# Scaling and biasing the attention scores on TensorE, and spreading the chunk inversion over four quadrants

## The reference

```
# RWKV-7, per head and direction, step by step
sa = S a_t
S  = S * w_t + sa b_t^T + v_t k_t^T
y_t = S r_t

# attention of one head, latent queries; context queries have keys of context only and no bias
s_loc = q k_r^T * scale + bias          # 64-wide rows, a mask of -1e9 outside a window
s_ctx = q k_ctx^T * scale
p = softmax([s_loc, s_ctx]);  o = p [v_r; v_ctx]
```

## Time and profile before

| | |
|---|---|
| Median of three runs | 2026.12 us (2019.57 to 2027.88) |
| The profiled execution's own time | 2030.75 us |
| Its span in the trace | 2028.6 us |
| TensorE busy | 1905.9 us, 94% |
| VectorE, ScalarE, GpSimd busy | 1001.8, 939.8 and 944.0 us (49%, 46%, 47%) |
| Mean granted TensorE clock | 0.982 of full speed |
| The chain that ended last | TensorE 79%, VectorE 9%, ScalarE 4% |

### The profile page before, as it was taken

How to read it: one execution, slowest core, us unless ns; L and a number is a source line. 1 busy time by engine, 2 the same in 40 slices (tenths; PEclk the granted TensorE clock), 3 DMA queues, 4 the chain that set the end, 5 groups by cost and what they waited for, 6 DMA issues and landing times.

```text
span 2028.6 us, 41739 instructions
## 1 busy us (share of the span) xinstructions
PE 1905.9 (94%) x17940; PEld 1718.9 (85%) x17940; DVE 1001.8 (49%) x1516; ACT 939.8 (46%) x1766; POOL 944.0 (47%) x767
## 2 busy tenths in 40 slices
PE   6899999999999989999988999999999998999997
PEld 2887878797899879999947878787879997899996
DVE  2574747475611255552057657475745133555502
ACT  4554645454533454443345555364554334544432
POOL 1434426170666626666416153342516664466663
PEclk9999999999999989999989999999999999999998
DMA  7314232232443314434453141413224432244442
GB/s 291 101 50 143 64 117 94 89 115 86 135 124 122 120 63 124 124 122 127 123 204 124 50 140 55 136 65 125 87 88 156 125 125 83 94 125 125 125 125 73
DMA packets 65414, 231.52 MB, mean 114 GB/s; under 512 B 7376, under 2 KB 11856, under 8 KB 64592
## 3 DMA queue, kind: packets, MB, share of 16 engines
q1 hardware_dynamic: 59040, 215.21, 33.3%
q10 hardware_dynamic: 6192, 13.66, 1.9%
HBM read 223.58 MB, written 5.26 MB: 113 GB/s over the span
## 4 chain that ended last, share of the span: by engine, by line
PE 79%; DVE 9%; ACT 4%; issue 3%; POOL 2%; DMA 2%; ACTq 1%; SPq 0%; DVEq 0%; POOLq 0%
PE psz L471 57%; PE psw L471 20%; DVE work L1360 3%; ACT work L954 3%; DMA ring<-in_w 2%; POOL ringlo L1735 1%; DVE work L1369 1%; PE psz L479 1%; PE psw L479 1%; ACT whi L954 1%; DVE rstd L1369 1%; DVE part L1360 1%; DVE work L1363 1%; POOL work L1771 1%; DVE work L1366 0%
## 5 line engine op out<-in xcount | busy, mean ns | idle before, releaser
L1735 POOL TENSOR_TENSOR ringlo<-ring,whi 128x512 fp32r<-128x512 f32 x608 | 811.1, 1357 | 756.7 <-ACT whi L954 756.7
L471 PE MATMUL psz<-hhi,whi 128*128 128x386 f32 x1696 | 587.1, 346 | 23.2 <-POOL ringlo L1735 14.5
L471 PE MATMUL psz<-hlo,whi 128*128 128x386 f32 x1696 | 577.6, 341 | 0.0
L471 PE MATMUL psz<-hhi,ringlo 128*128 128x386 f32 x1696 | 576.4, 340 | 0.0
L954 ACT ACTIVATE whi<-ring 128x1024 fp32r<-128x1024 f32 x304 | 320.2, 1053 | 133.4 <-PE psz L471 125.1
L471 PE MATMUL psw<-work 64*64 64x64 f32 (+4 forms) x9024 | 348.8, 232 | 17.6 <-issue 9.1
L471 PEld LDWEIGHTS psw<-work 64*64 64x64 f32 (+2 forms) x9024 | 294.5, 137 | 73.1 <-issue 55.6
L471 PEld LDWEIGHTS psz<-hhi,whi 128*128 128x128 f32 x1696 | 321.0, 189 | 36.1 <-issue 18.9
L471 PE MATMUL psz<-part,whi 128*128 128x386 f32 x1344 | 346.6, 339 | 3.2 <-DVE work L1360 1.5
L471 PEld LDWEIGHTS psz<-hlo,whi 128*128 128x128 f32 x1696 | 322.9, 190 | 2.1
L471 PEld LDWEIGHTS psz<-hhi,ringlo 128*128 128x128 f32 x1696 | 321.0, 189 | 0.0
(11 more groups left out here) (107 smaller groups left out, 1725.2 us busy)
## 6 DMA issues: line engine op xcount, KB each, us to landing
ring<-in_w SPq DMA_DIRECT2D x400, 512.0 KB, 3.5
pk<-in_pk ACTq DMA_DIRECT2D x8, 832.0 KB, 4.4
const<-in_const SPq DMA_DIRECT2D x1, 1795.0 KB, 10.0
work<-in_x SPq DMA_DIRECT2D x1, 1544.0 KB, 6.8
work<-in_x ACTq DMA_DIRECT2D x1, 1544.0 KB, 6.5
out_x<-work ACTq DMA_DIRECT2D x1, 1544.0 KB, 5.5
work<-out_x ACTq DMA_DIRECT2D x1, 1544.0 KB, 9.8
out_x<-work SPq DMA_DIRECT2D x4, 386.0 KB, 2.3
```

The source lines that it names most:

```text
L471: ins = nc.tensor.matmul(out, a, b, start=start, stop=stop, skip_group_check=True)
L1735: L.do(G.tensor_tensor(out, a, b, op), S[sig] if sig else None)
```

## The change

Two changes are made together.

**Attention.** The bias is added by a product of the identity with the bias, accumulated on the scores in PSUM, so that the scores need not be copied to SBUF: VectorE takes the negated maximum of bank 4 in one operation and ScalarE takes the exponential from bank 4. Bank 4 is free for the next job's scores only then (`p_ready` in the place of `s_ready`). The rows are no longer scaled: ScalarE multiplies the identity by the inverse row sums (`rdiag`, one buffer of 128x128, signal `ridiag_ready`), and TensorE turns the exponentials by a product with that matrix.

**Inversion.** Head 1's matrices in `tvv`, `g0` and `art` lie in swapped halves, so that the four products of an `x` (two heads, two chunks) take four different quadrants, and the loops over `x` and `hb` change places. The product waits for both heads at once. Step 3 of level 5 has a diagonal form in both heads. The transpose of a level is in three pieces: 128x384 for head 0 and two of 64x384 across the halves for head 1 (`across`); before level 1, `across` is added behind the transpose. The `art` copies on ScalarE are three in the place of one. `values(1)` and `powers(3)` on ScalarE change places.

```diff
                             else:
-                                pe.wait_ge(*at_of("s_ready", p, j - 1))
+                                pe.wait_ge(*at_of("p_ready", p, j - 1))
...
-                                mm(w(4, P, 256), q, nk[rows(hb), LAT:TP], sig="sc_done")
+                                mm(w(4, P, 256), q, nk[rows(hb), LAT:TP], True, False)
+                                if j == 1:
+                                    pe.wait_ge(*at_of("bias_ready", p, 0))
+                                a = PK["bias"] + 384 * hb + (P if kind == 1 else 0)
+                                mm(w(4, P, 256), ident, pk[:, a:a + 256], False, True, "sc_done")
...
-                            pe.wait_ge(*at_of("pn_ready", p, j))
+                            pe.wait_ge(*at_of("ridiag_ready", p, j))
...
-                                tr(w(5, i * P, P), scores[j % 2][:, i * P:(i + 1) * P], "pt_done" if i == n - 1 else None)
+                                mm(w(5, i * P, P), scores[j % 2][:, i * P:(i + 1) * P], rdiag,
+                                   sig="pt_done" if i == n - 1 else None)
...
-                            for hb in range(2):
-                                pe.wait_ge(*at_of("x_ready", p, 0 if lv == 1 else 2 * (lv - 2) + hb + 1))
-                                for x in range(6):
+                            pe.wait_ge(*at_of("x_ready", p, 0 if lv == 1 else 2 * (lv - 2) + 2))
+                            for x in range(6):
+                                for hb in range(2):
                                     for c in range(2):
-                                        mm(psw[hc(c), g_bank(lv, hb), CH * x:CH * x + CH], au[hc(c), hb, x, 0, 0:CH],
+                                        mm(psw[hc(c ^ hb), g_bank(lv, hb), CH * x:CH * x + CH], au[hc(c), hb, x, 0, 0:CH],
...
+                                        e = c ^ hb
+                                        o_ = psw[hc(e if lv == LEVELS - 1 else c), x_bank(lv, hb), CH * x:CH * x + CH]
+                                        mm(o_, a_[hc(e), hb, x, :], b_[hc(e), hb, x, :],
+                                           sig="xt_done" if (x, c) == (5, 1) else None)
...
-                            if i < 6:
-                                act.wait_ge(*at_of("sc_done", p, i))
-                                run(scores[i % 2][:, 0:P], w(4, 0, P), sig="sctx_ready")
+                            if 1 <= i <= 6:
+                                j = i - 1
+                                act.wait_ge(*at_of("ri_ready", p, j))
+                                run(rdiag, ident, ACT.Copy, "ridiag_ready", scale=ri[:, j % 2:j % 2 + 1])
...
-                        powers(3)
                         values(1)
+                        powers(3)
...
+                    def across():
+
+                        for c in range(2):
+                            flip(tvv[hc(1 - c), 1:2], xv[hc(c), 1:2], "tv_ready" if c else None)
...
-                                ts(s_[:, 0:n], s_[:, 0:n], ri[:, j % 2:j % 2 + 1], sig="pn_ready")
...
-                                flip(tvv, xv, "tv_ready")
+                                flip(tvv[:, 0:1], xv[:, 0:1])
+                                across()
```

More of the change, by code:

```diff
@@ L258, in trunk @@
         st = wk(3 * 256).rearrange("p (n s d v) -> p n s d v", n=3, s=2, d=2)
-        fin = wk(2 * 64).rearrange("p (d v) -> p d v", d=2)
+        rdiag = wk(P)
         lwal, lgl = wk(TP), wk(TP)
@@ L767, in _ @@
                                     ada_steps(2)
[L768 to L773, removed]
+                            pe.wait_ge(*at_of("gl_ready", p, lv - 1))
+                            pe.wait_ge(*at_of("tv_ready", p, lv - 1))
+                            a_, b_ = (gg, tvv) if lv == LEVELS - 1 else (tvv, gg)
+                            for x in range(6):
+                                for hb in range(2):
                                     for c in range(2):
[L775 to L776 removed]
+                                        e = c ^ hb
+                                        o_ = psw[hc(e if lv == LEVELS - 1 else c), x_bank(lv, hb), CH * x:CH * x + CH]
+                                        mm(o_, a_[hc(e), hb, x, :], b_[hc(e), hb, x, :],
+                                           sig="xt_done" if (x, c) == (5, 1) else None)
                             if lv <= 4:
@@ L784, in _ @@
                         freed(zb + 14)
-                        for hb in range(2):
-                            pe.wait_ge(*at_of("tv_ready", p, 4 + hb))
-                            for x in range(6):
+                        pe.wait_ge(*at_of("tv_ready", p, 6))
+                        for x in range(6):
+                            for hb in range(2):
                                 for c in range(2):
[L789 to L792, removed]
+                                    mm(psw[hc(c), hb, CH * x:CH * x + CH], tvv[hc(c ^ hb), hb, x, :],
+                                       art[hc(c ^ hb), x // 3, x % 3, rows(hb)], sig="wm_done" if (x, c) == (5, 1) else None)
+                        for x in range(6):
+                            for hb in range(2):
                                 for c in range(2):
-                                    mm(psw[hc(c), 2 + hb, CH * x:CH * x + CH], tvv[hc(c), hb, x, :],
-                                       g0[hc(c), hb, x, :], sig="u_done" if (x, c) == (5, 1) else None)
+                                    mm(psw[hc(c), 2 + hb, CH * x:CH * x + CH], tvv[hc(c ^ hb), hb, x, :],
+                                       g0[hc(c ^ hb), hb, x, :], sig="u_done" if (x, c) == (5, 1) else None)
                         retain(2)
@@ L1119, in powers @@
                                 act.wait_ge(*at_of("mx_ready", p, i))
-                                s_ = scores[i % 2][:, 0:384 if JOBS[i][1] else P]
-                                run(s_, s_, ACT.Exp, "p_ready", bias=mx[:, i % 2:i % 2 + 1], accum_out=rs[:, i % 2:i % 2 + 1])
+                                n = 384 if JOBS[i][1] else P
+                                run(scores[i % 2][:, 0:n], w(4, 0, n), ACT.Exp, "p_ready", bias=mx[:, i % 2:i % 2 + 1], accum_out=rs[:, i % 2:i % 2 + 1])
                         def retain(i):
@@ L1207, in _ @@
                                     seen(zi)
-                                    run(art[:, d], z(zi, 384).rearrange("p (t c) -> p t c", t=3), free=zi)
+                                    a = z(zi, 384).rearrange("p (t c) -> p t c", t=3)
+                                    run(art[:, d, :, rows(0)], a[:, :, rows(0)])
+                                    run(art[hc(0), d, :, rows(1)], a[hc(1), :, rows(1)])
+                                    run(art[hc(1), d, :, rows(1)], a[hc(0), :, rows(1)], free=zi)
                             elif lv in (2, 3):
@@ L1372, in pred, with flip @@
                         L.do(V.copy_predicated(out, mask, data), S[sig] if sig else None)
-                    def flip(out, a, sig):
-                        L.do(V.transpose(out.rearrange("p h x c -> p (h x c)"), a.rearrange("p h x c -> p (h x c)")), S[sig])
+                    def flip(out, a, sig=None):
+                        L.do(V.transpose(out.rearrange("p h x c -> p (h x c)"), a.rearrange("p h x c -> p (h x c)")),
+                             S[sig] if sig else None)
+                    def across():
+                        for c in range(2):
+                            flip(tvv[hc(1 - c), 1:2], xv[hc(c), 1:2], "tv_ready" if c else None)
                     def normed(j):
```

38 lines of the change are left out of this document (13 added, 25 removed).

## The result

The changed kernel takes 2071.21 us (median of 4 runs, 2068.53 to 2079.16), against 2024.42 (4 runs) for the one before on the same chip: 1.0239 times as long over all the runs, 95% interval 1.0202 to 1.0277 (the two medians alone give 1.0231). The forecast was 2062, with an own range of 2046 to 2076, and slower by over 0.5% at 0.85. The profiled execution took 2068.97 us, with a span of 2067.2.

What follows compares the result with a forecast made beforehand. TensorE's queue was taken as the bound. Terms 0.97 + 3.1 - 0.3 + 0.5 + 0.75 - 0.9 gave 4.1 us per pass, 33 for eight; on 2030.75, less 4.6, plus 3 for the clock: 2062 us, range 2046 to 2076.

Steps and rivals of the forecast that it cites:

- TensorE's ring: Each level is a TensorE, VectorE, ScalarE ring of 4.6 to 7.1 us; set savings count only where TensorE ends it.
- Four quadrants, 0.78 us a set: In eleven sets per pass, 24 products take 0.78 us instead of 1.54, a gain of 0.76 each.
- The rival in which two row halves cannot share a bank: Sets stay at 1.54 us because such products do not run together: 2092 us, chance 0.03.
- Level 1: First distance of a pass: ScalarE's rdiag waits for VectorE's inverse behind the transposes; 7.08 grows to 10.2 us, +3.1.
- the mark: Start of VectorE's transposes, one before level 1 and one at the end of levels 1 to 4.
- Levels 2 to 5: Per pass: level 2 -0.3 us, level 3 +0.5, level 4 +0.75, level 5 and two sets behind it -0.9.
- the dense part: Where TensorE is full, two bias products and one turned block come in: +0.97 us per pass.
- The clock: After level 1's idle stretch TensorE's granted clock may fall, costing up to 3 us; one or two falls, 3 us counted.
- the case of most passes: Rival: the clock falls in most passes, 2059 and 8 x 3 giving 2083 us, chance 0.13.
- The rival that TensorE stays the bound: rdiag does not hold up TensorE and quadrants pay: 1985 us, or 2009 with lost overlap; chance 0.09.
- its bar of 7.1 us: Level 1, mark to mark, must stay under 7.1 us for the rival that TensorE stays the bound.
- The rival in which it cancels: Cheap transposes and a shorter stall leave level 1's loss equal to gains elsewhere: 2020 to 2035 us, chance 0.06.

Runs made afterwards that it cites:

- The fillers: Changed kernel plus six products nobody reads, in TensorE's two gaps of level 1: 2060.47 us, 1.0175 against the kernel before.
- the queue in the new order: Job 2's inverse and decay tables ahead of masks, attend(3) ahead of across(): changed kernel 2020.39 us; inversion alone, without that inverse move but values(1) ahead of powers(3), 2001.86.

## Why the prediction was right

**TensorE's ring.** Held. The chain went from TensorE to ScalarE and VectorE, in level 1 above all.

**Four quadrants, 0.78 us a set.** Held: the weight loads of 48 records span 0.79 us, and the next product starts 0.86 behind the first. The rival in which two row halves cannot share a bank fell: each head's products from both row halves go to one bank (to different halves of its partitions), and a set takes 0.86. The 25 ns between starts that the Trainium skill ("TensorE: Matmul & The Clock Gate", "Wait — 56ns, not 53.3ns?") gives as a floor would make 1.2 us of a set. It does not hold across quadrants: within a group of four, records start 6 to 7 ns apart.

**Level 1.** The mechanism was right step by step, as these distances from the mark show (forecast, then measured): three transposes 2.15, 2.19; inverse done 2.34, 2.38; `rdiag` done 2.7, 2.8; the load begun 4.0, 3.74; job 4's scores begun 5.9, 5.55; next mark 10.2, 9.73. The stages of ScalarE's queue overlap by some 0.1 us each, which I had left out and which outweighs a longer `rdiag` (0.40 for 0.27); the two predicated copies took 1.06 for 1.2. Placing one instruction earlier took the stall away, and that shows the cause. The price of 2.66 us for a table load, from the Trainium skill ("ScalarE: Activation LUTs", "What ACT_TABLE_LOAD costs"), does not appear: in the changed kernel, too, the load begins 0.02 behind the end of the copy (128.80 to 128.82) and the exponential 0.02 behind the load.

**Levels 2 to 5.** 5.48, 4.93 and 7.17 against 5.5, 5.1 and 7.0. The last mark to the 16 products behind the sets is 163.31 - 155.03 = 8.28, against about 8.3. Each was within 0.2 us. In the dense part between passes 3 and 4, from the 16 products behind the sets to the next first mark, it is 78.81 us after (400.72 to 479.53) and 77.87 before (383.54 to 461.41): +0.94, against +0.97. Of the other stretches, the two in which the clock fell in neither kernel gave +0.53 (behind pass 5) and +0.95 (behind pass 7).

**The clock: the step that was mis-sized.** I allowed one or two falls, 3 us in all, and gave the case of most passes 0.13 and 24 us. It fell in level 1 in seven passes of eight, for 91.66 - 8 x 9.73 = 13.8 us, 1.6 to 2.5 a pass and not "up to 3". So the number of falls was that of the rival, each at less than its 3 us, and the time lay between the two cases. The fillers show that it is the clock and not the wait: with the same stall, 9.76 in all passes.

**What cancelled.** Four levels at full clock grew by 29.0 us, against 32.4 forecast; the clock in the levels 15 against 3; the rest -5.4 against +0.6. Of the last, 0.9 lie ahead of the first mark and 1.2 behind the last level; the stretches between the levels of one pass and the next within a layer take 86.5 to 90.4 us in both kernels, with slow clock behind some pairs, as in the earlier trace rows, and were not taken apart further. Against the profiled execution's own time the forecast was 2064 + 3, and 2068.97 came out, 2 us more. The median lies 9 off: those 2, the 4.6 that I took off because the profiled execution before was slower than its runs, and 2.2 by which the profiled one after was faster than its own. That the profiled total came within 2 us is in part luck: the forecast had the levels 3.4 us and the rest 6.0 us too high, and the slow clock 12 us too low. The marks are where it was right by its reasoning.

**The rival that TensorE stays the bound.** It fell as it was put: level 1 was above its bar of 7.1 us. The order of VectorE's queue was a part of it. With the queue in the new order the quadrants are worth 22 us in the whole change, yet that kernel takes 2020.39 with 7.24 us in level 1, still above the bar and outside the 1985 to 2009 of this rival. The inversion's part alone reaches 2001.86, but that is half of the change, and the rival spoke of all of it. The rival in which it cancels (2020 to 2035) fell too.

**What stays open.** Why the clock falls behind one gap and not behind a like one in another pass (the seventh here), and why it went to level 4 when level 1 was filled.

## What to carry to other kernels

When a change gives one engine more to do, look in that engine's queue for the small operation behind the new work that another engine is waiting for: here two transposes of 0.6 us each ahead of one reciprocal of 0.16 us held up three engines, and moving the reciprocal gave back 33 us. Make the two halves of a change separately: here one of them costs time in either order of the queue, and the other pays once the order is right. Read their queues again once one wait is gone, since a second chain may end at the same place. And count TensorE's gaps as well as its work: a gap costs its length, and here up to 2.5 us more in the slow clock behind it.

## What the runs showed of the hardware that was not expected

- A transpose on VectorE costs by its columns: three pieces with 384 columns each (one over 128 partitions, two over 64) take 1.79 us, 0.57 to 0.58 each, where one of 768 takes 0.98. Splitting one by partitions saves nothing.
- A set of 64x64 products with two quadrants in use or with four has the same distance of 58 to 59 ns between its groups of starts; four quadrants have twice the products in a group.
- 128x128 `rdiag`, out of SBUF and scaled by a column, took ScalarE 0.40 us, where a plain copy of 128x128 out of PSUM takes 0.28 (before, at 130.11); the exponential out of PSUM took 0.37, about as from SBUF (0.40).
- TensorE's clock fell to 0.50 behind gaps of 2 us with work between them in seven passes, and not in the remaining one, the seventh, with the same gaps. Filling the gaps kept it at 1.00 there, and it then fell three levels later in five passes.
